# A two-block model kernel: the meta rows' projections packed, the recurrence's products moved to the first stage, and the join of the blocks rewritten

## What is computed

```python
# first block: h = [meta (16), x (512)]
proj = einsum('bld,de->ble', rmsnorm(h, g_mix), w_in)       # 7 groups of 512 columns
sb_q, sb_k, sb_v, hg_q, hg_f, hg_i, hg_g = split(proj)
o_sb = stick_breaking_attention(sb_q, sb_k, sb_v)            # 8 heads of 64
log_f = log(lb + (1 - lb) * sigmoid(hg_f))
k_in, q_in = (1 - lb) * sigmoid(-hg_f), silu(hg_q)
o_hg = hgrn2_chunked(q_in, k_in, hg_i, log_f)                # 4 heads of 128, chunks of 128
h = h + concat(norm(o_sb), norm(o_hg) * silu(hg_g)) @ w_out
h = h + hierarchical_moe(rmsnorm(h, g_ffn))                  # 32 experts, 2 per token
x = rmsnorm(h[:, 128:], g_final)                             # 512 tokens
# second block: projections, convolution, state space branch, gated mix, then a dense FFN
x = x + rms_norm(mix(rms_norm(x, mix_pre_g_2) @ w_in_2), ...)
x = x + rms_norm(ffn(rms_norm(x, ffn_pre_g_2)), ...)
```

## Time and profile before

| | |
|---|---|
| median of three runs | 2245.93 us |
| the profiled execution, its time | 2249.91 us |
| the same, its span | 2247.7 us |
| PE busy | 2044.9 us (91%) |
| DVE busy | 1361.6 us (61%) |
| ACT busy | 1065.4 us (47%) |
| POOL busy | 175.2 us (8%) |
| mean granted TensorE clock | 0.947 |
| first stage, its products | 20.8 to 210 us |
| attention | 211 to 308 us |
| recurrence | 308 to 362 us |
| expert loop | 445 to 992 us |
| join | 997 to 1039 us |

### The profile page before, as it was taken

The page is one execution under the profiler, slowest core; times in us unless marked ns, Lnnn a source line. Parts: engine busy times, 40 slices in busy tenths (PEclk is TensorE's granted clock), DMA queues, the critical chain, the costliest instruction groups (busy, mean ns, idle before and its releaser), DMA issues. The chain is left out here.

```text
span 2247.7 us, 25099 instructions
## 1 busy us (share of the span) xinstructions
PE 2044.9 (91%) x10173; PEld 1633.3 (73%) x10173; DVE 1361.6 (61%) x1510; ACT 1065.4 (47%) x1252; POOL 175.2 (8%) x130
## 2 busy tenths in 40 slices
PE   7999988788999999956999999988699988999997
PEld 6887677666666666635888888877478867888786
DVE  4112776588999888945298888877534453333223
ACT  4224623377888888834335444444242233322212
POOL 1000100002222222200000000000000000000000
PEclk9999899899999999985999999999899998999999
DMA  5120004289999999943333333322222213333221
GB/s 183 57 75 1 1 1 161 109 323 388 394 406 402 406 404 400 386 176 81 95 94 94 94 94 94 94 76 57 56 94 94 94 56 103 94 94 96 92 94 57
DMA packets 201776, 346.84 MB, mean 154 GB/s; under 512 B 13587, under 2 KB 149259, under 8 KB 184251
## 3 DMA queue, kind: packets, MB, share of 16 engines
q1 hardware_dynamic: 194171, 333.42, 42.4%
q0 software_dynamic: 5120, 8.40, 1.1%
q10 hardware_dynamic: 2368, 3.39, 0.5%
HBM read 340.91 MB, written 12.65 MB: 157 GB/s over the span
## 5 line engine op out<-in xcount | busy, mean ns | idle before, releaser
L1492 DVE TENSOR_TENSOR wlo_e<-raw_e,whi_e 128x2048 fp32r<-128x2048 f32 x190 | 431.5, 2288 | 57.5 <-ACT whi_e L1417 57.2
L1417 ACT CAST whi_e<-raw_e 128x2048 fp32r<-128x2048 f32 x188 | 359.5, 1915 | 75.2 <-PE pall L1568 46.8
L1789 DVE TENSOR_TENSOR w_lo<-w_raw,w_hi 128x2048 fp32r<-128x2048 f32 x89 | 203.8, 2290 | 288.9 <-ACT w_hi L1781 288.8
L48 PE MATMUL pall<-hT_hi,w_lo 128*128 128x512 f32 x864 | 345.6, 400 | 9.5 <-ACT xbc L2213 3.1
L1781 ACT CAST w_hi<-w_raw 128x2048 fp32r<-128x2048 f32 x89 | 169.4, 1904 | 386.7 <-PE pall L50 370.6
L49 PE MATMUL pall<-hT_lo,w_hi 128*128 128x512 f32 x864 | 340.2, 394 | 0.0
L50 PE MATMUL pall<-hT_hi,w_hi 128*128 128x512 f32 x864 | 339.5, 393 | 0.0
L1567 PE MATMUL pall<-whi_e,xs 128*128 128x512 f32 x512 | 209.7, 410 | 3.1 <-DVE xs L1497 3.1
L1568 PE MATMUL pall<-wlo_e,xs 128*64 128x512 f32 x512 | 205.8, 402 | 0.0
L48 PEld LDWEIGHTS pall<-hT_hi,w_lo 128*128 128x128 f32 x864 | 164.8, 191 | 45.9 <-issue 4.8
L50 PEld LDWEIGHTS pall<-hT_hi,w_hi 128*128 128x128 f32 x864 | 164.6, 191 | 35.0
(11 more groups left out here) (468 smaller groups left out, 3804.1 us busy)
## 6 DMA issues: line engine op xcount, KB each, us to landing
raw_e<-in_w_expert_up_dram SPq DMA_DIRECT2D x64, 1024.0 KB, 10.3
raw_e<-in_w_expert_down_dram SPq DMA_DIRECT2D x64, 1024.0 KB, 11.0
raw_e<-in_w_expert_gate_dram SPq DMA_DIRECT2D x64, 1024.0 KB, 10.4
w_raw<-in_w_in_dram SPq DMA_DIRECT2D x80, 512.0 KB, 6.1
w_raw<-in_w_gate_up_dram SPq DMA_DIRECT2D x44, 512.0 KB, 5.1
w_raw<-in_w_down_dram SPq DMA_DIRECT2D x22, 512.0 KB, 4.1
mixed<-in_w_in_dram SPq DMA_DIRECT2D x10, 1024.0 KB, 5.1
A<-acs_rows SPq DMA_DIRECT2D x8, 1024.0 KB, 5.0
```

What stands on the lines that cost most here:

```text
L48: nc.tensor.matmul(out, w_lo, m_hi, start=start, stop=False)
L1417: nc.scalar.copy(whi[j], raw[j]).then_inc(sem_hi, 1)
L1492: nc.vector.tensor_tensor(wlo[j], raw[j], whi[j].bitcast(F32), ALU.subtract).then_inc(sem_lo, 1)
L1789: (engine or self.nc.vector).tensor_tensor(self.lo[i][:, :], self.raw[i][:, :], self.hi[i][:, :].bitcast(F32), ALU.subtract).then_inc(self ...
```

## The change

**Meta rows packed.** `aT_hi` and `aT_lo` lose their fifth tile. The 16 meta rows, turned, stand in `mT`: 16 columns hi and 16 columns lo, side by side. They are now the stationary operand, and the weights of k, v, hf and hi stream over them behind the unit's own products (`meta_part`): hi weights over all 32 columns, lo weights over the 16 hi columns. The 32 sums are copied to `meta_rows` by ScalarE, and a full-float product with `sel` (two identities, one above the other) adds the two halves and, for k and hf, turns them (`meta_turn`). ScalarE copies the result out (`meta_out`).

**Recurrence prepared in the first stage.** `forget` runs on ScalarE in the first unit of hi, `q1` and the decay products on GpSimd as soon as the gates are there, `keys` on VectorE behind the last subtraction. Several temporary tensors share memory for that.

**Join.** h is not normalized twice. With g the first gain, the rows h\*g are made; one pass squares h, a second squares h\*g, and a root over both sums gives the scale of the second norm at once. The first norm's rows are made on ScalarE at the end (`rows_out`). Four PSUM bank pairs take the place of one. The gains, and the second block's first two weight units with their hi and lo parts, are loaded and made at the end of the expert loop, whose places 4 and 5 are now the second block's own weight buffers; its hi places 0 to 3 are the later `hT`.

The order of the second block's instructions is as before.

```diff
@@ stage_a @@
+            mT = sb("mT_a", [P, KD, 2 * META], F32R, ctx=tmp)
+            msb = sb("meta_rows", [2 * META, 512], ctx=tmp)
+            sel = sb("sel", [2 * META, META], ctx=tmp)
@@ stage_a, GpSimd @@
+                pool.wait_ge(s["mask"], 1)
+                pool.wait_ge(s["f"], HG_HEADS)
+                nc.gpsimd.tensor_tensor(q1[:, :, :], hqT[:, :, :], hfT[:, :, META:TM], ALU.mult).then_inc(s["q1"], 1)
+                for i, w in enumerate(WIDE):
+                    if i >= 1:
+                        pool.wait_ge(s["dec"], i)
...
             @block.scalar
...
+                    if half == 0 and u >= 1 and units[u - 1][1] in META_OF:
+                        if u + 2 < len(units):
+                            make_hi(u + 2)
+                        meta_out(units[u - 1][1])
+                        if units[u - 1][1] == "hf":
...
+                            for e in range(HG_HEADS):
+                                forget(e)
+                        continue
+                    if half and what in META_OF:
+                        meta_sums(META_OF[what], u)
...
             @block.vector
...
                 for u in range(2, len(units)):
                     make_lo(u)
...
+                for e in range(HG_HEADS):
+                    keys(e)
...
             @block.tensor
...
+                def meta_part(what, half, wh, wl):
+                    if half == 0 and META_OF[what] >= 1:
+                        pe.wait_ge(s["ms"], META_OF[what])
...
+                    for k in range(wh.shape[1]):
...
+                        nc.tensor.matmul(MB[0:2 * META, c], mT[:, kk, :], wh[:, k, :], start=st, stop=False, skip_group_check=True)
+                        last = nc.tensor.matmul(MB[0:META, c], mT[:, kk, 0:META], wl[:, k, :], start=False, stop=sp_,
+                                                skip_group_check=True)
+                    return last
...
+                def meta_turn(what):
+                    m = META_OF[what]
+                    pe.wait_ge(s["ms"], m + 1)
...
+                    if what in ("k", "hf"):
+                        for e in range(4):
+                            last = nc.tensor.matmul(MT[:, e * META:e * META + META], msb[:, e * P:e * P + P], sel[:, :], start=True,
+                                                    stop=True)
+                    else:
+                        last = nc.tensor.matmul(MT[0:META, :], sel[:, :], msb[:, :], start=True, stop=True)
...
-                                if is_meta_turned(what):
-                                    nc.tensor.matmul(bm[:, 0:META], w_l, m_hi, start=st, stop=False)
-                                    nc.tensor.matmul(bm[:, 0:META], w_h, m_lo, start=False, stop=False)
-                                    nc.tensor.matmul(bm[:, 0:META], w_h, m_hi, start=False, stop=sp_)
...
+                    if half == 0 and u >= 1 and units[u - 1][1] in META_OF:
+                        meta_turn(units[u - 1][1])
+                    if what in META_OF:
+                        meta_part(what, half, wh, wl).then_inc(s["wused"], 1)
@@ the expert loop: SP, then ScalarE @@
+            sp.dma_start(gains[:, 0, :], dram["g_final"].unsqueeze(0)[0].partition_broadcast(P)).then_inc(g["s_gains"], 16)
+            sp.dma_start(gains[:, 1, :], dram["mix_pre_g_2"][0].partition_broadcast(P)).then_inc(g["s_gains"], 16)
+            sp.wait_ge(*made_lo(E - 2, 4))
+            sp.wait_ge(*made_lo(E - 3, 5))
+            for u in range(2):
+                W.load(sp, u)
...
             y_out(E - 2)
+            act.wait_ge(*used(E - 2, 4))
+            W.make_hi(act, 0)
+            W.make_hi(act, 1)
             y_out(E - 1)
@@ join: ScalarE, then VectorE @@
+            def roots(i):
+                act.wait_ge(s["sum"], 2 * i + 2)
+                nc.scalar.activation(sq[:, :], h[:, i, :], ACT.Square, accum_out=ssq1[:, i:i + 1]).then_inc(s["sq1"], 1)
+                act.wait_ge(s["hg"], i + 1)
...
+                nc.scalar.activation(sq[:, :], hg[:, i, :], ACT.Square, accum_out=ssq2[:, i:i + 1]).then_inc(s["sq2"], 1)
+                act.wait_ge(s["v"], i + 1)
+                nc.scalar.activation(rt12[:, i:i + 1], v[:, i:i + 1], ACT.Sqrt, bias=eps2[:, 0:1], scale=1.0 / D)
...
+            def rows_out(i):
+                act.wait_ge(s["r1"], i + 1)
+                nc.scalar.activation(h[:, i, :], hg[:, i, :], ACT.Copy, scale=rs1[:, i:i + 1]).then_inc(s["x"], 1)
+
+            roots(0)
+            for i in range(1, NT):
+                roots(i)
+                turned_hi(nc, act, s, i - 1, banks, hT[0], 2 * i - 2)
+            turned_hi(nc, act, s, NT - 1, banks, hT[0], 2 * NT - 2)
             for i in range(NT):
...
+                rows_out(i)
...
             joined(0)
             joined(1)
+            both(0)
             normed(0)
             joined(2)
+            both(1)
             normed(1)
+            turned_lo(nc, dve, s, 0, banks, *hT, 0)
             joined(3)
```

276 lines of the change are left out of this document (155 added, 121 removed).

## The result

The changed kernel takes **2233.05 us** (median of six runs, 2221.16 to 2235.64), the kernel before 2248.13 us (six runs, 2241.59 to 2252.52). The ratio is 0.9928, with an interval of 0.9900 to 0.9955. It is faster, as forecast, but by some 15 us and not by 26, and 3 us outside the range. The profiled execution took 2235.64 us (span 2233.9).

The account below looks back on a forecast made before the run. DMA bounds the expert loop, TensorE the first stage, the VectorE-ScalarE chain the join; the attention loses time to a stall and half clock. Gains 14.1 + 11.4 + 0.5 = 26.0 us off 2245.9 give 2220 us, range 2213 to 2230.

Parts of the forecast that it names:

- Packed meta rows, 14.1 forecast: First stage: 33.3 us of meta-row products on TensorE go, 19.2 us are added; gain 14.1 us.
- rival of narrow products as dear as wide ones: First stage: 256-column products cost what 512-column ones do, 0.23 us each; 2227 us in all; chance 0.10.
- Attention, 11.4 forecast: Attention: moving GpSimd's work to the first stage removes an excess of 5.0 + 6.35 us; gain 11.4 us.
- The stall and its cause: Attention: VectorE's cast and subtraction slow beside GpSimd's products; TensorE sits idle 2.40 us on the subtraction.
- in the attention this removes the stall and with it the clock drop: Attention: without GpSimd's work there, both TensorE's wait and the half clock behind it go; gain 11.4 us.
- the clock falls in the attention anyway: Rival, attention: one clock drop remains and its half-clock part of 6.35 us stays; 2226 us; chance 0.12.
- Hidden work: First stage: the moved scalings and GpSimd's 10.5 us lie under TensorE's work and cost nothing.
- rival of the lock that moves along: First stage: weight subtractions meet GpSimd work, TensorE idles, its clock falls, another 6.4 us; 2228 us; chance 0.08.
- Expert loop, zero forecast: Expert loop: added loads and roundings at its tail fit in ScalarE's idle 5.84 us; zero, bound 2 us if late.
- Join, 0.5 forecast: Join: VectorE starts 2.7 us earlier, but TensorE starts at 1039.0 where it started at 1039.55; gain 0.5 us.
- the early start is given back at the end: Join: the 2.7 us earlier start is lost again by the stage's end, leaving 0.5 us.
- my walk: Join: chain of roots at 1011.6, 1017.9, 1025.5 and 1029.8, ScalarE's output rows until 1038.7, TensorE at 1039.0.

Follow-up runs that it names:

- Experiment 3: Changed kernel with padding around or behind the first stage's transposed activations: 64 bytes twice, 2225.14 us; 960 bytes, 2229.53 us; 1984 bytes, 2220.54 us.
- experiment 4: Changed kernel with ScalarE's output rows in the join made earlier, only one left at the end: 2229.17 us (one run).
- after_again: The changed kernel, unchanged, run again for a second profile: 2223.44 us.

## Why the prediction was right and wrong

*Packed meta rows, 14.1 forecast, 11.3 seen.* The terms were right: 64 narrow products at 0.114 us (7.3; booked 7.7), 32 wide ones at 0.233 (7.5; 7.4), four turns at 0.96 to 0.99 (3.9; 4.1), 18.7 in sum against 19.2. The rival of narrow products as dear as wide ones is refuted, and all evacuations stayed hidden: no wait of TensorE between the third unit and the attention. The step that failed is one I never wrote down: that the products which stay keep their pitch, 0.227 us. They did not: 384 of them start 0.233 us apart and 288 start 0.229 apart. Experiment 3 gives the cause, the place of the buffers, and the price. From the second unit's first product to the attention's first it took 176.2 us before, 164.8 after, and 162.3 with the padding. So the packing gives 13.9 of the 14.1 us, and the place takes 2.5 back. (33.3 less 18.7 would be 14.6. Some 0.4 of the difference stands ahead of the four turns, where the next product starts 0.33 us later and not 0.23.) By the same pitch, the first unit's 48 products would add some 0.3, an estimate. What moved the weight buffers by 1088 bytes modulo 2048 was the new small tensors ahead of them.

*Attention, 11.4 forecast, 3.3 seen in the means.* The stall and its cause were right, and it went with the move. The step "in the attention this removes the stall and with it the clock drop" took 5.0 + 6.35 us of one execution as a property of the code. What the move takes away in every profile is the wait: 87.91 - 85.42 = 2.5 us. The half clock behind it is there in two of five profiles, at 8 to 9 us (96.78 and 95.71 against 87.91). And I named "the clock falls in the attention anyway" as a rival at 0.12, for 6.35 us, when a drop at the attention's start is the more frequent of the two over all profiles (twelve of seventeen, 3.2 or 4.8 us). That rival, and not the forecast, is what happened, at another place than I gave it. In the means the kernel before lost 4.3 us less than in its first profile (92.5 against 96.8), and the changed kernel 3.7 us more than its 85.4 without a drop (89.1): together the 8.1 us that are missing.

*Hidden work.* GpSimd's products, the forget scalings and the keys cost nothing in the first stage: TensorE has no gap there. The rival of the lock that moves along did not happen, and was hardly tried: GpSimd works from 167.80 to 177.7 us, and VectorE's subtractions of weights, 2.29 us each, fall before and behind it:

```profile
164.37 2.29 DVE L375 TENSOR_TENSOR wlo_a<-mixed,whi_a 128x2048 fp32r<-128x2048 f32 x1 [10.29 <-ACT whi_a L266]
178.13 2.29 DVE L375 TENSOR_TENSOR wlo_a<-mixed,whi_a 128x2048 fp32r<-128x2048 f32 x1 [11.46 <-ACT whi_a L266]
```

*Expert loop, zero forecast, -0.6 seen.* The means hide a spread of 11 us (537.8 to 549.1 in eighteen profiles) which goes with one gather. GpSimd's gather behind the first scatter took 11.64 us in the changed kernel's first profile, and TensorE waited 10.3 us for token rows there; in after_again it took 2.50. GpSimd's timeline in the one and in the other:

```profile
495.68 11.64 POOL L1048 DMA_INDIRECT xg<-m_rows,row_x  x1 [0.30 <-issue]
```

```profile
491.13 2.50 POOL L1048 DMA_INDIRECT xg<-m_rows,row_x  x1 [0.31 <-issue]
```

Seven profiles have a gather of 11.6 us and loops of 545.1 to 549.1, seven have none over 3 us and loops of 537.8 to 544.8; both kernels are in both groups. The four others have one of 7.2 us and loops of 541.6 to 544.5. Why it is slow in some runs stays open: nothing was tried on it.

*Join, 0.5 forecast, 4.2 seen.* Of the 4.2, 1.1 is the long stage end of the first profile of before, spread over three. The rest: VectorE starts 12.5 to 13.5 us after the last evacuation instead of 15.8 to 16.3, as forecast (2.7), and the step "the early start is given back at the end" is what failed. From VectorE's first sum to TensorE's first product my walk gave 36.0 us (1003.0 to 1039.0); it takes 33.76, and took 33.80 before. I had tile 3's root 1.9 us too late (26.8 us after the first sum; 24.9 measured), and the output rows behind it moved with it. That the four rows of ScalarE set the end was right, as experiment 4 shows.

*The number.* The changed kernel comes near 2220 when nothing falls in: after_again, without a slow gather, took 2223.44, 3.2 of it for the short drop at the attention's start. One of the six runs took 2221.16, but it has no profile. That this is close to the forecast is luck in part, since 2220 was added up without the 2.5 us of the pitch and with 3.7 too little for the join. The range was built from the bounds of the terms and the spread of three runs; the spread of nineteen runs of the kernel before was 2238.81 to 2260.81.

## What to carry to other kernels

A stretch at half clock in one profile is not yet a cost of the code: book the wait that is there in every profile, and take a second profile before you book the clock behind it. A small new tensor moves all buffers that lie behind it, so compare the pitch of the untouched products too. Where TensorE pauses, look at what it does next: a few dense products in the pause or right behind it can pay for themselves.

## What was not expected of the hardware

- The pitch of products of equal shape at a granted clock of 1.00 depends on where the operands lie in SBUF: 0.227 us with activations and weights 0 or 1024 bytes apart modulo 2048, 0.229 to 0.234 at 1088 and 1152. Two fast and two slow places don't make a rule, and whether it is the distance of the two operands or the place of one of them was not tried apart. The Trainium skill, page "TensorE: Matmul & The Clock Gate", section "Back-to-back issue gap", gives the gap of a single product by the number of columns alone, 518 cycles or 0.216 us for 512 when warm, and some 0.131 us for a sustained stream; the fastest stretch above has 0.227, so the trace is above both figures at every place.
- The clock falls after a pause of 0.94 us, with TensorE fully busy at that moment, and stays up after one of 2.38 us (three of five profiles). In the second block it falls without a pause, while TensorE is busy without a gap in a run of 96 products of 32 columns: in all eighteen profiles, 2.4 to 5.8 us behind the first of them. So a pause is not needed. Busy time by stretch in the changed kernel, whose run of 96 goes from 1039.51 to 1055 us:

```profile
1044.00:1048.00 4.00, 4.00 (x24) 4.00 (x23) 2.09 (x1) 0.00 (x0) 0.00 (x0) 0.58 0.00 0
1048.00:1052.00 4.00, 4.00 (x21) 4.00 (x20) 0.00 (x0) 0.00 (x0) 0.00 (x0) 0.50 0.00 0
```
